# Weight tables in places of 64 tokens with earlier fetches, and the 64 tokens' sums of rows moved from TensorE to VectorE and GpSimd

## The reference, cut to what matters

```
q  = (h2 @ wq).reshape(t, 8, 2, 128)              # 8 heads, two halves
va, ia = top_k(q[:, :, 0] . keys[0], 16);  vb, ib = top_k(q[:, :, 1] . keys[1], 16)
top, pos = top_k(va + vb over all 16 x 16 pairs, 16);  eidx = 128 * ia + ib of the chosen
g = softmax(top)
a = gelu(sum_d u_tab[eidx, d] * h2[t, d])
out[t] = sum over the 8 x 16 chosen of  g * a * v_tab[eidx]
```

## Time and profile before

| | |
|---|---|
| median of 3 runs | 2589.88 us (2587.07 to 2590.89) |
| the profiled execution, its own time | 2589.13 us |
| its span in the profile | 2587.4 us |
| TensorE busy / VectorE / ScalarE / GpSimd | 2334.6 (90%) / 1586.1 (61%) / 869.6 (34%) / 850.6 us (33%) |
| mean granted TensorE clock | 0.952 |

### The profile page before, as it was taken

One profiled execution on the slowest core, in us unless ns is written; L12 is line 12 of the kernel. 1 busy time (PEld: TensorE's weight loads), 2 busy tenths in 40 slices (PEclk: granted clock), 3 DMA queues, 4 the chain that ended last, 5 costly groups with the idle time before them and its releaser, 6 DMA issues.

```text
span 2587.4 us, 32955 instructions
## 1 busy us (share of the span) xinstructions
PE 2334.6 (90%) x13072; PEld 1790.2 (69%) x13072; DVE 1586.1 (61%) x3185; ACT 869.6 (34%) x1617; POOL 850.6 (33%) x648
## 2 busy tenths in 40 slices
PE   8999988997987777779899966799999999999999
PEld 7756555675544444368677865688888888888887
DVE  5358567453100000054537989699889888889986
ACT  3134333432000000033424348544433333333332
POOL 0013221001110010000004548365567776666760
PEclk9999898998999999969998967899999999999999
DMA  5345010246999999842005117999999999999993
GB/s 192 126 173 195 33 66 33 101 182 236 427 426 426 426 426 426 339 164 98 33 33 204 41 47 246 359 409 342 349 406 413 414 413 413 382 403 399 400 396 126
DMA packets 141711, 693.69 MB, mean 268 GB/s; under 512 B 18428, under 2 KB 45092, under 8 KB 107760
## 3 DMA queue, kind: packets, MB, share of 16 engines
q1 hardware_dynamic: 80816, 479.68, 46.6%
q0 software_dynamic: 60736, 211.85, 21.0%
HBM read 659.52 MB, written 38.81 MB: 270 GB/s over the span
## 4 chain that ended last, share of the span: by engine, by line
PE 64%; DVE 17%; DMA 15%; ACT 2%; issue 1%; SPq 0%; DVEq 0%; POOLq 0%; ACTq 0%
PE psum L3606 14%; DMA arena<-w 13%; PE psum L3571 12%; PE psum L2236 4%; PE psum L470 4%; PE psum L986 4%; PE psum L1707 3%; PE psum L3577 2%; DVE arena L3821 2%; PE psum L3575 2%; PE psum L1287 2%; PE psum L1302 2%; DVE rounded L3704 2%; PE psum L2387 2%; DVE arena L3291 1%; PE psum L3529 1%
## 5 line engine op out<-in xcount | busy, mean ns | idle before, releaser
L3606 PEld LDWEIGHTS psum<-rounded,rounded 128*128 128x128 f32 x2880 | 432.0, 189 | 29.9 <-ACT rounded L3653 11.7
L3606 PE MATMUL psum<-rounded,rounded 128*128 128x320 f32 x2880 | 445.0, 311 | 7.1 <-DVE rounded L3704 6.2
L3571 PE MATMUL psum<-rounded,rounded 128*128 128x512 f32 x1536 | 398.7, 396 | 2.7 <-DVE rounded L3724 2.3
L3517 POOL DMA_INDIRECT arena<-u_rows,arena x192 | 283.5, 1476 | 180.0 <-DVE arena L3821 57.2
L3571 PEld LDWEIGHTS psum<-rounded,rounded 128*128 128x128 f32 x1536 | 283.4, 189 | 80.0 <-issue 14.3
L3517 POOL DMA_INDIRECT arena<-v_rows,arena x192 | 288.6, 1503 | 152.4 <-DVE arena L3832 66.8
L3704 DVE TENSOR_TENSOR rounded<-arena,rounded 128x1024 fp32r<-128x1024 f32 x248 | 303.0, 1222 | 6.6 <-ACT rounded L3639 6.6
L1707 PE MATMUL psum<-arena 128*64 128x256 f32 x2048 | 234.5, 384 | 59.5 <-DMA arena<-w 58.8
L1835 DVE COPY arena<-psum 128x256 f32<-128x256 f32 x32 | 13.6, 425 | 407.3 <-PE psum L1774 407.3
L3639 ACT ACTIVATE rounded<-arena 128x1024 fp32r<-128x1024 f32 x248 | 260.0, 1049 | 8.6 <-DMA arena<-uv 7.7
L1707 PEld LDWEIGHTS psum<-arena 128*64 128x64 f32 x2048 | 148.7, 138 | 156.4 <-DMA arena<-w 63.1
(11 more groups left out here) (515 smaller groups left out, 3782.6 us busy)
## 6 DMA issues: line engine op xcount, KB each, us to landing
arena<-w SPq DMA_DIRECT2D x96, 2048.0 KB, 42.4
arena<-uv SPq DMA_DIRECT2D x124, 1024.0 KB
arena<-wada SPq DMA_DIRECT2D x12, 2048.0 KB
gd<-arena SPq DMA_DIRECT2D x19, 1024.0 KB, 9.3
arena<-gd SPq DMA_DIRECT2D x30, 640.0 KB
arena<-wp SPq DMA_DIRECT2D x8, 2048.0 KB
arena<-win SPq DMA_DIRECT2D x4, 2048.0 KB
arena<-wq SPq DMA_DIRECT2D x4, 2048.0 KB
```

Source lines behind the costliest of these rows:

```text
L3517: po.indirect_dma_start(out=ROWS_OF[i % len(ROWS_OF)], out_offset=None, in_=src, in_offset=bass.IndirectOffsetOnAxis(ap=column.bitcast(U32 ...
L3571: ins = pe.matmul(PS[:, 2 * n + half, :], gg[:, z, 128 * n:128 * n + 128], v[:, y, 512 * half:512 * half + 512], x == 0 and i == 0, x == 1 ...
L3606: ins = pe.matmul(PS[:, 7, 0:DT], w[:, y, k, :], hv[:, z, :], k == 0 and i == 0, k == 7 and i == 2)
```

## The change

It has two parts.

1. **The tables.** They are written from two places of 64 tokens (8,192 words each), `g_of(x)`, x = 0 to 4. Three quarters of a place that held a table of 128 tokens become free. So H, the first three raw pieces and the hidden rows `H2S` are fetched at once behind product 7; the products lie in `FP` from the start and aren't written and read back; their GELUs run on ACT in quads 34 to 41; H's upper parts run on ACT in quads 50 to 53, its lower parts on GpSimd (before: VectorE) in quads 51 to 54; split 0 runs on ACT in quad 54 and on GpSimd in quad 56. The first weights `G_FIRST` (192 of the tokens) are fetched during the gather stage. GpSimd's first eight gathers no longer wait for TensorE's `rows`. In the keys stage the units 5 and 6 go to places that come free only after the last chunk of queries, unit 7 after product 1; their splits run behind the scores of chunk 15, on GpSimd ahead of `sums(6)`.
2. **The 64 tokens' sums.** `gather_round`, `few_weights`, the masks W32 and the turned list of rows go. 64 "few sums" of 128x1024 on VectorE take their place, in units 63 to 235, with 64 gathers as before. The splits of every fourth unit, 16 to 236 (56 of them), go from VectorE to GpSimd (`by_pool`).

The core of the diff:

```diff
-    FU = [o, 0, 2048, 2 * RING, 2 * RING + 2048, 3 * RING, 3 * RING + 2048, RING]
+    FU = [o, 0, 2048, 2 * RING, 2 * RING + 2048, RING, RING + 2048, 0]
-    FP = [at(RING + 2048 + DT * i, DT) for i in range(6)] + [at(DT * i, DT) for i in range(2)]
-    es = nc.dram_tensor("es", [128, 8 * DT], F32, kind="Internal").ap()
+    FP = [at(3 * RING + DT * i, DT) for i in range(8)]
-    FIRST_SPLIT = {4: 0, 6: 1, 7: 2, 10: 3, 11: 4, 13: 5, 14: 6}
+    FIRST_SPLIT = {4: 0, 6: 1, 7: 2, 10: 3, 11: 4}
...
 (keys_sp)
-                sp.wait_ge(*K.pe["q", x - 1, 3])
+                sp.wait_ge(*(Y.pe["product", 1] if x == 4 else K.pe["q", 3 if x == 3 else x - 1, 3]))
...
 (keys_ac)
         scores(15)
+        first_split(5)
+        first_split(6)
+        out_first(ac, 0)
+        out_first(ac, 1)
         first_split(7)
...
 (keys_po)
+        first_rest(5)
+        first_rest(6)
         sums(6)
         first_rest(7)
...
+    EARLY_SPLIT, GELU_AT, H_AT = 54, 34, 50
+    def g_of(x):
+        o = 0 if x % 2 else O_TEMP
+        return AR[:, o:o + 8192].rearrange("p (a t r) -> p a t r", a=32, r=4)
...
 (gather_ac)
+                if 0 <= q4 - GELU_AT < 8:
+                    u = q4 - GELU_AT
+                    ac.activation(FP[u], FP[u], ACT.Gelu_apprx_tanh).then_inc(*E.ac("gelu", u))
...
 (gather_po)
+                if 0 <= q4 - H_AT - 1 < 4:
+                    y = q4 - H_AT - 1
+                    hv = hs_parts(y)
+                    po.wait_ge(*G.ac["h", y])
+                    po.tensor_tensor(hv[:, 1], H2R[:, 2 * y:2 * y + 2, :], hv[:, 0].bitcast(F32), ALU.subtract).then_inc(*G.po("h", y))
+                if q4 == EARLY_SPLIT + 2:
+                    po.wait_ge(*E.ac["split", 0])
+                    po.tensor_tensor(SPL[0][:, 1024:2048], at(RAW[0], 1024), SPL[0][:, 0:1024].bitcast(F32), ALU.subtract).then_inc(
+                        *G.po("split"))
...
 (dense)
+        FEW_SUMS.setdefault(63 + 175 * k // FEW, []).append(k)
-    ROUND = {63 + 175 * r // 31: r for r in range(ROUNDS)}
+    def by_pool(j):
+        return j % 4 == 0 and 16 <= j < 240
+    def split_done(j):
+        return E.po["split", j] if by_pool(j) else E.dv["split", j]
...
 (dense_po: the gathers as before, one queue with the splits)
+        def split(j):
+            s = SPL[j % 5]
+            po.wait_ge(*E.ac["split", j])
+            po.tensor_tensor(s[:, 1024:2048], at(RAW[(j // 2) % 3] + 1024 * (j % 2), 1024), s[:, 0:1024].bitcast(F32),
+                             ALU.subtract).then_inc(*E.po("split", j))
+        for i in range(len(ROWS_OF)):
+            gather(i)
+        i = len(ROWS_OF)
+        for j in range(len(UNITS)):
+            if j + AHEAD < len(UNITS) and by_pool(j + AHEAD):
+                split(j + AHEAD)
+            while i < len(ROWS_IN_TURN) and ROWS_IN_TURN[i - len(ROWS_OF)][2] < j:
+                gather(i)
+                i += 1
...
 (dense_dv)
+        for x in range(4):
+            product(x)
         wait_all(dv, G)
+        product_end(0)
+        product_end(1)
         split(1)
...
-            if j + AHEAD < len(UNITS):
+            if j + AHEAD < len(UNITS) and not by_pool(j + AHEAD):
                 split(j + AHEAD)
...
+            for k in FEW_SUMS.get(j, []):
+                row, there = rows_of("few sum", k)
+                dv.wait_ge(*there)
+                if k:
+                    dv.wait_ge(*E.dv["few sum", k - 1])
+                    dv.scalar_tensor_tensor(H2T2, row, Z2[:, k:k + 1], H2T2, ALU.mult, ALU.add).then_inc(*E.dv("few sum", k))
...
-            if j + 2 in ROUND:
-                ...
-                dv.scalar_tensor_tensor(W32[r % 4], ...)
 (fold_few)
-            for k in range(4):
-                ins = pe.transpose(PS[:, 6, 128 * k:128 * k + 128], H2T2[:, 128 * k:128 * k + 128], IDENT)
+            for k in range(8):
+                ins = pe.matmul(PS[:, 6, 64 * k:64 * k + 64], H2T2[:, 128 * k:128 * k + 128], BOTH, True, True)
```

More of the change, by code:

```diff
@@ L2867, in keys_ac @@
         scores(15)
+        first_split(5)
+        first_split(6)
+        out_first(ac, 0)
+        out_first(ac, 1)
         first_split(7)
-        for u in range(4):
-            out_first(ac, u)
+        out_first(ac, 2)
+        out_first(ac, 3)
         wait_all(ac, K)
@@ L3377, in build @@
     for j in range(len(UNITS)):
[L3378 to L3382, removed]
-    ROW_NO = {x: i for i, x in enumerate(ROWS_IN_TURN)}
+        ROWS_IN_TURN += [("few dot", k, j) for k in FEW_DOTS.get(j, [])]
+        ROWS_IN_TURN += [("dot", k, j) for k in DOTS.get(j, [])]
+        ROWS_IN_TURN += [("sum", k, j) for k in SUMS.get(j, [])]
+        ROWS_IN_TURN += [("few sum", k, j) for k in FEW_SUMS.get(j, [])]
+    ROW_NO = {(x, k): i for i, (x, k, j) in enumerate(ROWS_IN_TURN)}
     def unit(kind, x):
         return UNITS.index((kind, x))
+    def by_pool(j):
+        return j % 4 == 0 and 16 <= j < 240
+    def split_done(j):
+        return E.po["split", j] if by_pool(j) else E.dv["split", j]
     def rows_of(*x):
@@ L3505, in dense_po @@
                 was, before, _ = ROWS_IN_TURN[i - len(ROWS_OF)]
-                po.wait_ge(*(E.pe["round", before] if was == "round" else E.dv[was, before]))
+                po.wait_ge(*E.dv[was, before])
             if (kind, k) == ("dot", 0):
@@ L3519, in dense_po @@
                 *d_rows[i % len(ROWS_OF)]("row", i))
[L3521 to L3531 removed]
+        def split(j):
[12 more added lines that the diff above has]
+                i += 1
+        assert i == len(ROWS_IN_TURN)
+    def dense_pe(pe):
         def rows_of_hidden(name):
@@ L3620, in dense_pe @@
             for x in TAIL:
-                pe.wait_ge(*E.dv["split", unit("v", x)])
+                pe.wait_ge(*split_done(unit("v", x)))
                 pe.wait_ge(*E.dv["gg", x])
@@ L3656, in dense_ac @@
         split(2)
-        ac.wait_ge(*d_first.end())
-        product(0)
-        product(1)
-        upper(0, gated(0))
-        product(2)
-        product(3)
-        upper(1, gated(1))
-        for x in range(4, 8):
-            product(x)
-            if x < 6:
-                upper(x - 2, gated(x - 2))
+        for x in range(4):
+            upper(x, gated(x))
         for j, (kind, x) in enumerate(UNITS):
@@ L3688, in dense_ac @@
                 ac.activation(Z2 if few else ZS, Z2 if few else ZS, ACT.Gelu_apprx_tanh).then_inc(*E.ac("z", WEIGHTS[j]))
-            if FOLD.get(j + 1) == "few":
-                ac.wait_ge(*E.pe["round", ROUNDS - 1])
-                ac.wait_ge(*E.dv["few dot", FEW - 1])
-                ac.activation(H2T2[:, 0:512], PS[:, 6, :], ACT.Copy).then_inc(*E.ac("few sum"))
         ac.wait_ge(*E.dv["sum", REST - 1])
+        ac.wait_ge(*E.dv["few sum", FEW - 1])
         for n in (0, 2, 1):
@@ L3817, in dense_dv @@
             for k in FEW_DOTS.get(j, []):
-                row, there = rows_of("few dot", k, 0)
+                row, there = rows_of("few dot", k)
                 dv.wait_ge(*E.ac["few rows"])
@@ L3822, in dense_dv @@
             for k in DOTS.get(j, []):
-                row, there = rows_of("dot", k, 0)
+                row, there = rows_of("dot", k)
                 dv.wait_ge(*E.ac["rows"])
@@ L3827, in dense_dv @@
             for k in SUMS.get(j, []):
-                row, there = rows_of("sum", k, 0)
+                row, there = rows_of("sum", k)
                 dv.wait_ge(*there)
```

225 lines of the change are left out of this document (82 added, 143 removed).

## The result

The changed kernel takes 2637.08 us (median of 4 runs, 2634.59 to 2640.07); the kernel before took 2590.39 beside it (4 runs, 2587.07 to 2591.44). The ratio is 1.0175, with a 95% interval of 1.0158 to 1.0191: the change makes the kernel slower by 46.7 us. The forecast was 2649 us, with a range of 2615 to 2700. The profiled execution took 2638.09 us, with a span of 2636.4.

The account below looks back on a forecast made before the run. TensorE bounds the kernel now, with VectorE close behind; after the change VectorE would. 2589.1 + 55 (dense loop) + 5 (coupled queues) + 0 (seam) = 2649 us, with 8 in 10 for 2615 to 2700.

Parts of the forecast that it names:

- The block: Dense loop: each GpSimd split holds up VectorE's instructions with two SBUF inputs for 2.2 us, 1.1 us per pair.
- the mean of VectorE's own splits: Dense loop, a sign of being right: L3704's mean rises above 1.22 us, some ending just behind a GpSimd split.
- The beat: Dots and sums: VectorE, not TensorE, sets the time of a pair, 8.08 us and 8.25 us against 7.64.
- The dense loop: Dense loop: +19 us in the dots, +28 in the sums, +8 in units 16 to 47; coupling +5 more.
- two queues that wait for each other: Dense loop: nearly full VectorE and GpSimd queues lose 0.05 us per pair, 5 us.
- Units 8 to 47: Units 16 to 47: a split moved saves 1.22 and blocks 2.2 us, +0.49 x 16 pairs = +8 us.
- The seam: From gather stage to dense loop: early fetches' gains are offset by later work, 0 +/- 5 us.
- `sums(6)`: Keys stage: it comes later than VectorE wants it, behind two `first_rest`; the path slips 2.2 us.
- No block: Rival, dense loop: VectorE isn't held up and TensorE stays the bound, 2560 us; chance of faster 0.12.
- GpSimd starves: Rival, dense loop: GpSimd's splits run only when VectorE stops, +65 to +90, 2725 us; chance with the clock 0.08.
- No change: Rival, dense loop: the block costs half, 1.1 us each, about 2587 to 2592 us; chance 0.03.
- The clock: Rival: TensorE idles about 1 us in 8; 2.4 GHz expected to hold, a fall meaning the upper end; with starving 0.08.

Follow-up runs that it names:

- e5: e1 plus two idle GpSimd tensor_tensor of 128x512 at each of 46 units, which nobody waits for; 2671.33 us, ratio 1.0302.
- e10: The changed kernel with GpSimd's splits from unit 56 on alone, 46 in place of 56; 2623.38 us, ratio 1.0134.
- e1: The changed kernel with every split back on VectorE, GpSimd only gathers; 2576.60 us, ratio 0.994.
- e11: e5 with each idle GpSimd tensor_tensor replaced by a tensor_copy of 128x512, which reads one operand from SBUF; 2613.35 us, ratio 1.0089.
- e4: The changed kernel with 63 of the 64 few sums on 8 of 1,024 columns, GpSimd's splits kept; 2584.87 us, ratio 0.9958.
- e9: The changed kernel with the 32 rounds back on TensorE in place of the few sums, every fourth unit's split on GpSimd; 2605.70 us, ratio 1.0048.
- e8_twice_first: e7_keys_order with VectorE's copy `twice` moved from unit 0 to right behind the gather stage's end; 2573.81 us, ratio 0.9924.
- e7_keys_order: e1 with GpSimd's `sums(6)` ahead of `first_rest(5)` and `first_rest(6)` in the keys stage; 2577.03 us, ratio 0.9944.
- e12_every_eighth: The changed kernel with every eighth unit's split on GpSimd in place of every fourth, 28 for 56; 2608.14 us, ratio 1.0060.

## Why the prediction was right, step by step

- **The block.** This carried the forecast: 2.2 us of VectorE for each GpSimd split. Measured: 2.2 from the longer instructions of after; 2.06 of the kernel's time for the two idle halves of e5; and the forecast's net price, 2.2 - 1.22 = 0.98 us a split, against 1.1 measured over all 56. The rule read from two places of the trace, the other's length less 0.2 us, held for three forms: 1.294 against 1.03, 0.615 against 0.42, and 2.35 (the shortest of L3515) against 2.2. One sign failed: the mean of VectorE's own splits should have risen and stayed at 1224 ns from 1800 us on; there dots, sums and `lower` took the block.
- **The beat.** Forecast 8.08 us in the dots and 8.25 in the sums, plus 0.05. From u49 to u69 (163.1 us, 20 pairs) it is 8.16, from u89 to u119 (247.0 us, 30 pairs) 8.23.
- **The dense loop.** The forecast's terms add up to +60 and 46.2 were measured; the difference is here. Forecast +52 from unit 48 on (19 + 28 + 5), measured -1.7 + 17.0 + 22.9 = +38. The term that was mis-sized is mainly the number of pairs: I took the full beat for 44 and 46. The first ten pairs of each stretch, u39 to u49 and u79 to u89, took 76.9 and 77.2 us, 7.7 a pair. VectorE may work ahead by three units and fourteen fetched rows, and has to use up that lead first; that this is the reason is argued from the beat alone. e10, which enters the dots without ten earlier GpSimd splits, takes 79.9 us for u39 to u49, but it has the halt behind the late transfers there, so it doesn't decide. The 5 us for two queues that wait for each other were too many: in the two windows VectorE idles only 0.2 and 3.0 us, so little was lost that way.
- **Units 8 to 47.** Forecast +8, measured +10.8 (+12.4 against e1). Part of it is one place: the first GpSimd split, of unit 16, stands behind gathers, and TensorE's matmuls wait 4.6 us for it (the last fence below); with the slower group behind the wait that is 7.3 us of the 12.4. That is GpSimd's queue, which I had priced at 0.05 us a pair, everywhere alike.
- **The seam.** Forecast 0 +/- 5, measured -3.5. `sums(6)` came late by 2.24 us (2.2 forecast). From the marker, GpSimd's last table part ends 9.5 us later than before (1632.84 - 1477.56 against 1620.60 - 1474.82), and `twice` is still used 1.6 us earlier (168.81 against 170.43), where I had 0.6. What I left out is the rest: from there to u9 TensorE takes 17.9 us, where it took 18.7, and u9 to u10 takes 7.20 us, where it took 8.26.
- **The rivals.** *No block* falls with e1, e5 and e11. *GpSimd starves* falls as the cause with e5, where nobody waits for GpSimd's work, and with e4 and e9; late splits still held TensorE up for 14.2 us in e4. *No change* through half a block falls with the longest dots (3982 ns, the whole block). *The clock* cost a few us in one place, below.

## What to carry to other kernels

Before work goes from VectorE to GpSimd, look at whether both read SBUF: VectorE's instructions with two SBUF inputs stood still here for GpSimd's operation less some 0.2 us, so a 1.22 us instruction saved cost 2.2 us, and the right move was the opposite one. GpSimd's memsets, which read nothing, were free. And where an engine is full only in a part of a loop, spread its side work over the units first: that gave more here (8 to 12 us) than the whole of part 1 (6 us).

## What the runs showed of the hardware that was not expected

- Being first doesn't spare VectorE. In the record at 2005.53 the dot begins 0.26 us ahead of GpSimd's split, and yet nearly all its work is done behind it. At 1702.71 in after, where GpSimd had begun 0.24 us earlier, a split takes 3.35 us. The Trainium skill (SBUF — State Buffer, "Who interferes with whom") says that the order of issue decides which of the two is blocked; by these records the start of an instruction's record doesn't give that order.
- A halt of 4.6 us brought TensorE's clock down. At unit 16 of the kernel after it stood from 1700.4 to 1705.0 us; then the granted clock is 0.55, the lower of the two levels (1.2 GHz), for one group: 24 matmuls take 6.35 us in place of 3.68. The windows, and the group in the timeline:

```profile
1690.00:1700.00 10.00, 10.00 (x53) 8.59 (x53) 9.27 (x17) 3.91 (x6) 8.10 (x7) 1.00 1.02 415
1700.00:1705.00 5.00, 0.41 (x2) 0.00 (x0) 4.69 (x7) 1.56 (x3) 4.42 (x3) 0.89 1.03 410
1705.00:1711.40 6.40, 6.36 (x25) 6.37 (x26) 1.75 (x4) 0.00 (x0) 4.56 (x4) 0.55 1.02 414
1711.40:1720.00 8.60, 8.60 (x47) 7.56 (x47) 8.07 (x10) 4.33 (x7) 6.35 (x4) 1.00 1.02 413
```

```profile
1705.04 6.35 PE L3598 MATMUL psum<-rounded,rounded 128*128 128x320 f32 x24 [4.62 <-POOL rounded L3515]
```

  So that one late split cost the wait and 2.7 us more. The length of the halt alone doesn't tell what follows: behind halts of 2.79 us (e1_all_dve, 1926 us) and 3.18 us (e9_rounds_pool_splits, unit 16) the group took 3.76 and 3.79 us, behind 2.85 us (e8_twice_first, 1931 us) and 3.10 us (e7_keys_order, 1927 us) it took 5.15 and 5.28, and behind 4.62 us at unit 16 of e12_every_eighth 5.32.
